# A hybrid encoder trunk on one core: another opening program, square sums one step later, set-up matrices at other places of the gate loop

## The chip, the cores and the metric

The kernel runs on one core of a Trainium2 chip. The metric is the device time of one execution in microseconds (us). TensorE multiplies, VectorE (DVE) and ScalarE (ACT) work on 128-partition tiles, GpSimd (POOL) does small side work, SyncE (SP) issues most DMAs. Each engine runs its own program in order and meets the others only at semaphores.

## The reference, cut to what matters

Two layers, 512 tokens, width 1024, all in float32.

```python
for l in range(DEPTH):                       # DEPTH = 2
    h = h + 0.5 * rms_norm(swiglu(rms_norm(h, g[0]), gate1, up1, down1), g[1])
    h = h + rms_norm(hybrid_mixer(rms_norm(h, g[2]), ...), g[3])
    h = h + 0.5 * rms_norm(swiglu(rms_norm(h, g[4]), gate2, up2, down2), g[5])

def rms_norm(x, g):
    return x * rsqrt(mean(x * x, -1) + 1e-6) * g
def swiglu(x, w_gate, w_up, w_down):         # 1024 -> 2816 -> 1024
    return (silu(x @ w_gate) * (x @ w_up)) @ w_down
```

The mixer has one input projection, a sliding-window attention, an S5 state-space layer, a forgetting attention, three branch norms and an output projection. The S5 layer's parameters are small: from `lam_re`, `lam_im`, `log_dt` it needs per state

```python
dt = exp(log_dt); mag = exp(min(lam_re, -1e-4) * dt)
ab_re = mag * cos(lam_im * dt);  ab_im = mag * sin(lam_im * dt)
z = ((ab_re - 1) + i ab_im) / (lam_re + i lam_im)      # scales B
```

The kernel turns them into matrices of powers of `ab`, so that the scan runs over chunks of 8 tokens. These matrices are made once per layer, beside the first FFN of the layer.

## The kernel before

**Layout.** Activations stand transposed: `hT[p, d, t]`, eight tiles d of 128 channels by 512 tokens. Every float32 product is made of three matmuls on split operands: a value is rounded to a high part (`xh`, `wh`, `Hh`) and a low remainder (`xl`, `wl`, `Hl`), and the product is xh·wh + xl·wh + xh·wl.

**A unit** is one weight tile: 1024 input channels by 128 output channels (512 KB). SyncE loads it into one of four raw slots. ScalarE rounds it (`split`, L914 to L918), VectorE makes the low part (`low`, L1334 to L1338), TensorE then runs its 24 matmuls (`unit_x`, L505, with L501 to L503 in `three`). A unit may be split when the unit two before it is done. Unit 2f of an FFN is the gate tile f, unit 2f + 1 the up tile f.

**The start of a stage.** `first_four` (L512) runs the first four units together, over the input tiles k as they come: `FIRST` lists (k tiles, units) for each step. Before its last two steps it runs `pre_norm` (L535): one fp32 matmul of ones with `acc`, the sum of the squares of h over the eight tiles, which ScalarE (`Square`, L955) and VectorE (`pre_sum`, L1355 to L1363) made. From it ScalarE makes `rstd` (`root`, L928 to L932). The input is not multiplied by `rstd`; the products are, in the gate function.

**The gate function** (`silu` on VectorE, L1405; `sigmoid` on ScalarE, L992) is a chain that goes back and forth between the two engines: L1407, ACT L996, L998, L1000, DVE L1411, ACT L1004, DVE L1416, L1418, then `times_up` L1423 with the up tile, ACT L1008 (`high`), DVE L1430 (`low_h`). The splits and lows of later units are placed between them by hand. In an FFN ramp unit 9's low half stands behind the fourth chain.

**Set-up of the S5 matrices** runs inside FFN 1 of each layer. GpSimd loads B and C, makes small powers and `bbar` and releases `z_bb` (`ssm_setup`). VectorE runs 12 `powers_step`s (L1456), each one instruction on 128x1024: they stand behind the pieces of `four` (L1474), the first at piece 10 (`POWER_AT`). TensorE runs six `ssm_matrix` steps (L555) behind the units of `STEP_UNIT`; ScalarE copies their results out (L967) three pieces later, at the end of the piece.

**The opening.** SyncE loads x as one DMA, then eight parameter transfers, then weights. TensorE waits for all of them, transposes x through PSUM (L491) and the parameters (L496, L497). ScalarE copies the eight tiles to `hT` (L898), converts two constants (L900, L901), and works on the S5 scalars with VectorE (L903 to L912, L1292 to L1331). Then both split the first four weight tiles, and make `xh` (L949) and `xl` (L1352).

## Time and profile before

Three timed runs took 2057.76 (median), 2057.37 and 2064.17 us. The profiled execution took 2057.29 us; its span, from the first to the last instruction that the profile counts, is 2055.5 us.

| engine | busy us | share of the span |
|---|---|---|
| TensorE (PE) | 1962.5 | 95% |
| VectorE (DVE) | 1128.1 | 55% |
| ScalarE (ACT) | 882.0 | 43% |
| GpSimd (POOL) | 208.8 | 10% |

A timeline row reads: start, duration, engine, line, operation, what is written and read, shape, count, and in brackets how long the engine was idle before it and what released it. Durations of pipelined instructions overlap, so the step from start to start is what counts. PEclk is TensorE's granted clock, 1.00 for 2.4 GHz and 0.50 for 1.2 GHz.

### The profile page before, as it was taken

How to read it: one execution, taken by the hardware profiler on the slowest of the kernel's cores; microseconds unless marked ns; L12 is line 12 of the kernel's file. 1: busy time of each engine (PE TensorE's matmuls, PEld its weight loads, DVE VectorE, ACT ScalarE, POOL GpSimd, SP SyncE). 2: the span in 40 equal slices, each digit the busy share in tenths (PEclk: the TensorE clock that was granted, in tenths of full speed). 3: DMA queues.
4: the chain of work that ended last, by engine and by line, in shares of the span. 5: the costliest groups of instructions: out<-in, count | busy, mean ns of one | idle time of the engine just before them, and what ended most of it. 6: DMA issues, size and time to landing. Idle time of an engine off the chain costs nothing.

```text
span 2055.5 us, 25149 instructions
## 1 busy us (share of the span) xinstructions
PE 1962.5 (95%) x9068; PEld 1565.1 (76%) x9068; DVE 1128.1 (55%) x1597; ACT 882.0 (43%) x1398; POOL 208.8 (10%) x409
## 2 busy tenths in 40 slices
PE   5999999999889999999999999999988999999997
PEld 4787888877657788888877788887765777888885
DVE  4674553377555755552277645325865576555323
ACT  4544442254554554442254444323555445444221
POOL 6502000012100000000057010000120000000000
PEclk9999999999989999999999999999999999999998
DMA  5324343252113233333332343333411123333321
GB/s 158 92 83 126 101 119 92 66 147 85 52 35 89 62 103 92 102 108 99 88 91 84 106 119 101 112 93 89 154 32 52 42 82 92 93 99 106 101 82 41
DMA packets 330427, 188.53 MB, mean 92 GB/s; under 512 B 6981, under 2 KB 325417, under 8 KB 329321
## 3 DMA queue, kind: packets, MB, share of 16 engines
q1 hardware_dynamic: 324520, 168.65, 28.5%
q0 software_dynamic: 5824, 18.79, 3.0%
q8 instruction: 50, 0.82, 0.2%
q14 instruction: 33, 0.26, 0.0%
HBM read 175.72 MB, written 11.67 MB: 91 GB/s over the span
## 4 chain that ended last, share of the span: by engine, by line
PE 74%; DVE 14%; ACT 8%; issue 3%; DMA 0%; SPq 0%; DVEq 0%; ACTq 0%
PE ps L501 13%; PE ps L502 13%; PE ps L503 13%; PE ps L632 8%; PE ps L634 8%; PE ps L633 8%; DVE wl L1337 3%; ACT wh L918 2%; DVE hT L1398 2%; PE ps L781 2%; PE ps L738 1%; DVE acc L1363 1%; PE ps L730 1%; DVE yF L1396 1%; ACT sig L998 1%
## 5 line engine op out<-in xcount | busy, mean ns | idle before, releaser
L1337 DVE TENSOR_TENSOR wl<-raw,wh 128x1024 fp32r<-128x1024 f32 (+1 forms) x270 | 356.3, 1320 | 519.5 <-ACT wh L918 518.3
L501 PE MATMUL ps<-xh,wh 128*128 128x512 f32 x1552 | 614.7, 396 | 11.0 <-DVE wl L1337 11.0
L502 PE MATMUL ps<-xl,wh 128*128 128x512 f32 x1552 | 607.5, 391 | 0.0
L503 PE MATMUL ps<-xh,wl 128*128 128x512 f32 x1552 | 607.5, 391 | 0.0
L918 ACT ACTIVATE wh<-raw 128x1024 fp32r<-128x1024 f32 (+1 forms) x270 | 304.9, 1130 | 443.7 <-PE ps L634 341.0
L501 PEld LDWEIGHTS ps<-xh,wh 128*128 128x128 f32 x1552 | 293.6, 189 | 80.5 <-DVE wl L1337 15.5
L503 PEld LDWEIGHTS ps<-xh,wl 128*128 128x128 f32 x1552 | 293.1, 189 | 62.3
L502 PEld LDWEIGHTS ps<-xl,wh 128*128 128x128 f32 x1552 | 293.7, 189 | 58.9
L632 PE MATMUL ps<-Hh,wh 128*128 128x512 f32 x704 | 278.3, 395 | 0.0
L634 PE MATMUL ps<-Hh,wl 128*128 128x512 f32 x704 | 278.0, 395 | 0.0
L633 PE MATMUL ps<-Hl,wh 128*128 128x512 f32 x704 | 277.9, 395 | 0.0
L632 PEld LDWEIGHTS ps<-Hh,wh 128*128 128x128 f32 x704 | 132.7, 189 | 32.4 <-DVE wl L1337 1.7
L634 PEld LDWEIGHTS ps<-Hh,wl 128*128 128x128 f32 x704 | 132.7, 188 | 31.0
L633 PEld LDWEIGHTS ps<-Hl,wh 128*128 128x128 f32 x704 | 132.7, 189 | 30.6
L1008 ACT ACTIVATE Hh<-full 128x512 fp32r<-128x512 f32 (+1 forms) x88 | 55.7, 632 | 228.0 <-DVE full L1423 217.5
L1411 DVE SCALAR_TENSOR_TENSOR sig<-sig 128x512 f32<-128x512 f32 x88 | 61.4, 697 | 130.2 <-ACT sig L1000 130.2
L996 ACT ACTIVATE sig<-sig 128x512 f32<-128x512 f32 x88 | 55.6, 632 | 147.3 <-DVE sig L1407 147.3
L1416 DVE TENSOR_TENSOR sig<-sig 128x512 f32<-128x512 f32 x88 | 62.0, 705 | 53.1 <-ACT sig L1004 53.1
L1004 ACT ACTIVATE sig<-sig 128x512 f32<-128x512 f32 x88 | 55.4, 630 | 57.8 <-DVE sig L1411 57.8
L1136 ACT ACTIVATE probT<-ps 128x256 f32<-128x256 f32 (+3 forms) x64 | 31.3, 489 | 84.6 <-PE ps L758 84.6
L1000 ACT ACTIVATE sig<-sig,ones 128x512 f32<-128x512 f32 x88 | 63.7, 724 | 2.9
L1418 DVE TENSOR_TENSOR sig<-sig,rstd 128x512 f32<-128x512 f32 x88 | 62.6, 712 | 3.0
(298 smaller groups left out, 2073.0 us busy)
## 6 DMA issues: line engine op xcount, KB each, us to landing
raw<-in_ffn_gate SPq DMA_DIRECT2D x88, 512.0 KB, 3.9
raw<-in_ffn_up SPq DMA_DIRECT2D x88, 512.0 KB, 3.9
raw<-in_ffn_down SPq DMA_DIRECT2D x64, 704.0 KB, 4.6
raw<-in_w_in SPq DMA_DIRECT2D x28, 512.0 KB, 4.0
raw<-in_w_out SPq DMA_DIRECT2D x16, 512.0 KB, 4.0
yF<-in_x SPq DMA_DIRECT2D x1, 2048.0 KB, 9.9
ssm_t<-evict POOLq DMA_DIRECT2D x8, 256.0 KB, 4.3
ssm_v<-evict POOLq DMA_DIRECT2D x8, 256.0 KB, 2.7
```

Of the source, the lines that this page charges most:

```text
L501: pe.matmul(bank, w_tile(True, slot, kw), xh[:, kx, :], start=first, stop=False)
L502: pe.matmul(bank, w_tile(True, slot, kw), xl[:, kx, :], start=False, stop=False)
L503: return pe.matmul(bank, w_tile(False, slot, kw), xh[:, kx, :], start=False, stop=last)
L632: pe.matmul(bank, wh[:, slot, k, :], Hh[:, f, :], start=(f == 0), stop=False)
L633: pe.matmul(bank, wh[:, slot, k, :], Hl[:, f, :], start=False, stop=False)
L634: mm = pe.matmul(bank, wl[:, slot, k, :], Hh[:, f, :], start=False, stop=(f == KF - 1))
L918: act.activation(w_high(slot, k0, nk), raw[:, slot4, 0:nk - k0, :], ACT.Copy).then_inc(w_hi, 1)
L1000: act.activation(e, e, ACT.Ln, bias=ones[:, 0:1]).then_inc(si_a, 1)
L1337: V.tensor_tensor(w_low(slot, k0, nk), raw[:, slot4, 0:nk - k0, :], w_high(slot, k0, nk).bitcast(F32), ALU.subtract).then_inc(w_split, 1)
L1411: V.scalar_tensor_tensor(e, g, 0.0, e, ALU.min, ALU.subtract).then_inc(si_v, 1)
L1416: V.tensor_tensor(e, g, e, ALU.mult).then_inc(si_v, 1)
L1418: V.tensor_tensor(e, e, rstd[:, :], ALU.mult).then_inc(si_v, 1)
```

## The change

- The first gate tile is loaded from ScalarE's queue. x comes in two halves, into memory of its own (`xrow`), with the gains and the identity between; weights 1 to 3 stand around the second half, and six late parameter transfers follow them.
- TensorE runs 12 small matmuls on constants first, transposes the gains and four tiles of x, and turns the other four tiles and the late parameters between the steps of a new order `FIRST0` of the first four units.
- ScalarE makes `xh` straight from PSUM; VectorE makes `xl` from PSUM and copies the tile to `hT`.
- The S5 scalars move: columns and angles on VectorE between the x tiles, the functions with their table loads and the two constant copies on ScalarE between weight split 4 and `root`, the inverse on VectorE behind the square sum, the 13 products to GpSimd. GpSimd's set-up of layer 0 starts when unit 0 is done.
- In all six ramps `pre_norm` stands before the last step in place of the last but one.
- The power steps start at piece 12 in place of 10; those of even pieces stand inside the gate function, behind `low_h`.
- ScalarE's matrix copies stand before the split of their piece in place of after its gate function or `high`.

```diff
-POWER_AT = 10
+POWER_AT = 12
+FIRST0 = (((0,), (0,)), ((0,), (1,)), ((1,), (0, 1)), ((0, 1), (2,)), ((2,), (0, 1, 2)), ((3,), (0, 1, 2)),
+          ((0, 1, 2, 3), (3,)), ((4,), (0, 1, 2, 3)), ((5,), (0, 1, 2, 3)),
+          ((6, 7), (0,)), ((6, 7), (1,)), ((6, 7), (2,)), ((6, 7), (3,)))
+X_TURN = {3: 4, 4: 5, 5: 6, 8: 7}
+P_TURN = 7
...
# SyncE
-            sp.dma_start(yF[:, :, :].rearrange("p (t a) n -> p t (a n)", t=TOK),
-                         x[0].rearrange("(t p) d -> p t d", p=P)).then_inc(s_in2, 16)
+            x_half(0)
+            sp.dma_start(par[0:96, 0, 0:P], norm_gains.rearrange("l g (k p) -> (l g k) p", p=P)).then_inc(s_in, 16)
             sp.dma_start(ident[:, :], const[:, K_ID:K_ID + P]).then_inc(s_in, 16)
...
+                    for i in range(4):
+                        if i == 2:
+                            x_half(1)
+                        if i:
+                            load(i, i, raw[:, i, 0:KD, :], columns((gate, up)[i % 2], l, slice(i // 2 * P, i // 2 * P + P)))
+                    late_params()
...
# TensorE
-            pe.wait_ge(s_in, 16 * 8)
-            pe.wait_ge(s_in2, 16)
+            pe.wait_ge(dve_c, 1)
+            for _ in range(SPIN_START):
+                pe.matmul(ps[0][:, 0:P], ones[:, :], ones[:, :], start=True, stop=True, skip_group_check=True)
+            def turn_x(k):
+                if k >= 4:
+                    pe.wait_ge(s_in2[1], 16)
+                    pe.wait_ge(h_new, k - 3)
                 if k == 7:
-                    pe.wait_ge(h_new, 1)
+                    pe.wait_ge(prm_rdy, 2)
...
+            def turn_params():
+                pe.wait_ge(s_set, 1)
+                pe.wait_ge(h_new, 4)
+                pe.transpose(ps[7][:, 0:R_C], par[0:R_C, 1, 0:P], ident[0:R_C, 0:R_C]).then_inc(s_set2, 1)
...
-                for step, (ks, us_) in enumerate(FIRST):
-                    if step == len(FIRST) - 2:
+                order = FIRST if s else FIRST0
+                for step, (ks, us_) in enumerate(order):
+                    if step == len(order) - 1:
                         pre_norm(s)
+                    if s == 0 and step in X_TURN:
+                        turn_x(X_TURN[step])
+                    if s == 0 and step == P_TURN:
+                        turn_params()
...
# ScalarE
+            act.dma_start(raw[:, 0, 0:KD, :], ffn1_gate[0:1, :, 0:P].rearrange("a (k p) f -> p (a k) f", p=P)).then_inc(landed[0], 16)
+            def ssm_functions():
+                act.wait_ge(s_ssm, 2)
+                act.activation(ssm[:, 4, :], ssm[:, 4, :], ACT.Exp).then_inc(s_act0, 1)
+                act.wait_ge(s_ssm, 3)
+                act.activation(ssm[:, 8, :], ssm[:, 7, :], ACT.Sin).then_inc(s_act0, 1)
+                act.activation(ssm[:, 9, :], ssm[:, 7, :], ACT.Sin, scale=0.5).then_inc(s_act0, 1)
+                act.add_instruction(mybir.InstLoadActFuncSet(...))
+                act.activation(ln_t[:, :], eps_t[:, :], ACT.Ln).then_inc(act_c, 1)
+                act.activation(maskb[:, :], maskf[:, :], ACT.Copy).then_inc(act_c, 1)
+                act.activation(identb[:, :], ident[:, :], ACT.Copy).then_inc(act_c, 1)
...
                 split_ahead(s, fourth(s) + 1)
+                if s == 0:
+                    ssm_functions()
                 act.wait_ge(pre_mm, s + 1)
                 root(ps[PRE_BANK][:, :], D_MODEL, rstd[:, :], ln_rdy, s * 2 + 1, pre_r)
...
                     for i in range(i0, 4):
+                        if i in step_of:
+                            ssm_matrix(l, step_of[i])
                         split(j * 4 + (n0 + i), j + n0 // 4, i, gu_slot(4 + i), KD)
...
-                        if i in step_of:
-                            ssm_matrix(l, step_of[i])
...
+            split_ahead(0, 0)
             act.wait_ge(prm_rdy, 1)
+            for k in range(KD):
+                x_start(k)
+                if k < 4:
+                    if k != 2:
+                        split_ahead(0, (1, 2, 0, 3)[k])
...
# VectorE
+            def x_start(k):
+                src = ps[4 + k % 4][:, :]
+                dve.wait_ge(x_hi, k + 1)
+                V.scalar_tensor_tensor(xl[:, k, :], src, prm[:, k:k + 1], xh[:, k, :].bitcast(F32),
+                                       ALU.mult, ALU.subtract).then_inc(x_rdy, 1)
+                V.tensor_copy(hT[:, k, :], src).then_inc(h_new, 1)
+            low_ahead(0, 0)
+            for k in range(KD):
+                x_start(k)
+                if k in (0, 1, 3):
+                    low_ahead(0, (1, 2, 0, 3)[k])
+                if k == 3:
+                    spread()
+                if k == 5:
+                    ssm_columns()
+            ssm_angles()
...
                 pre_sum(s)
+                if s == 0:
+                    ssm_inverse()
                 low_ahead(s, 4)
...
+                        def between():
+                            low_h(f + (tiles - 1), 1 - fb, bass.ds(f - 1, 1))
+                            if 0 <= step < 12:
+                                powers_step(step)
                         if i % 2 == 0:
                             dve.wait_ge(unit_done, n - 2 + SPLIT_SLOTS + 1)
-                            silu(f + tiles, b, lambda: low_h(f + (tiles - 1), 1 - fb, bass.ds(f - 1, 1)))
+                            silu(f + tiles, b, between)
                         else:
                             times_up(f + tiles, fb, b, n - 2)
-                        if set_up and 0 <= 4 * j + i - POWER_AT < 12:
-                            powers_step(4 * j + i - POWER_AT)
+                            if 0 <= step < 12:
+                                powers_step(step)
...
# GpSimd
-                if l:
-                    await_(unit_done, l * U_LAYER + SPLIT_SLOTS)
+                await_(unit_done, l * U_LAYER + SPLIT_SLOTS + 1 - (1 if l else 0))
...
                 if l == 0:
-                    await_(s_ssm, 4)
+                    ssm_products()
```

## Rows read from the trace of the kernel before

**Rows 1.** The page's chain by engine, and TensorE's waits (total us, times, longest).

```profile
PE 74%; DVE 14%; ACT 8%; issue 3%; DMA 0%; SPq 0%; DVEq 0%; ACTq 0%
...
PE ps L501 <- DVE wl L1337: 11.0, 13, 2.0
...
PE ps L538 <- DVE acc L1363: 4.9, 5, 1.0
...
PE ps L569 <- ACT evict L983: 4.0, 4, 1.4
```

**Rows 2.** Timeline of TensorE, 10 to 51 us (columns as told above).

```profile
12.19 1.12 PE L491 MATMUL ps<-ident,yF 128*128 128x128 f32 x4 [12.19 <-DMA full<-const]
...
29.18 0.77 PE L526 MATMUL ps<-xh,wh 128*128 128x512 f32 x1 [11.40 <-DVE wl L1337]
...
50.26 1.02 PE L538 MATMUL ps<-acc,ones 128*128 128x512 f32 x2
```

**Rows 3.** Timeline of ScalarE and VectorE, 18 to 42 us.

```profile
18.52 0.57 ACT L900 ACTIVATE maskb<-full 128x384 bf16<-128x384 f32 x1
...
19.76 0.21 ACT L905 ACTIVATE ssm<-ssm 128x16 f32<-128x16 f32 x1 [0.38 <-DVEq L1300]
...
21.67 1.28 ACT L910 ACT_TABLE_LOAD   x1
...
23.07 1.04 ACT L918 ACTIVATE wh<-raw 128x1024 fp32r<-128x1024 f32 x1
...
35.29 0.68 DVE L1360 TENSOR_TENSOR acc<-sq 128x512 f32<-128x512 f32 x1
...
36.66 4.68 DVE L1363 TENSOR_TENSOR acc<-acc,sq 128x512 f32<-128x512 f32 x6 [0.70 <-ACT sq L955]
```

**Rows 4.** Windows of SyncE: stretch, length, PEclk, DMA share, GB/s.

```profile
2.00:7.00 5.00, 1.00 1.02 329
...
12.00:18.00 6.00, 1.00 1.18 279
```

**Rows 5.** Timeline of TensorE in the ramps of the FFNs and behind the set-up.

```profile
82.37 0.50 PE L501 MATMUL ps<-xh,wh 128*128 128x512 f32 x1 [1.10 <-DVE wl L1337]
...
96.13 0.50 PE L501 MATMUL ps<-xh,wh 128*128 128x512 f32 x1 [1.99 <-DVE wl L1337]
...
194.00 0.39 PE L501 MATMUL ps<-xh,wh 128*128 128x512 f32 x1
...
199.44 0.39 PE L501 MATMUL ps<-xh,wh 128*128 128x512 f32 x1
...
713.62 0.50 PE L501 MATMUL ps<-xh,wh 128*128 128x512 f32 x1 [0.67 <-DVE wl L1337]
...
1055.25 1.13 PE L538 MATMUL ps<-acc,ones 128*128 128x512 f32 x2 [0.98 <-DVE acc L1363]
...
1100.38 0.50 PE L501 MATMUL ps<-xh,wh 128*128 128x512 f32 x1 [1.70 <-DVE wl L1337]
...
1198.70 0.39 PE L501 MATMUL ps<-xh,wh 128*128 128x512 f32 x1
```

**Rows 6.** Timeline of VectorE, 91 to 103 us: gate chain and power step.

```profile
91.00 0.69 DVE L1411 SCALAR_TENSOR_TENSOR sig<-sig 128x512 f32<-128x512 f32 x1 [1.52 <-ACT sig L1000]
...
93.72 1.22 DVE L1468 TENSOR_TENSOR prod<-bbar,pw_b 128x1024 f32<-128x1024 f32 x1
...
102.27 0.69 DVE L1411 SCALAR_TENSOR_TENSOR sig<-sig 128x512 f32<-128x512 f32 x1 [1.52 <-ACT sig L1000]
```

**Rows 7.** TensorE's small matmuls, and the window behind them (PE, PEld, DVE, ACT, POOL, PEclk).

```profile
176.13 4.21 PE L577 MATMUL ps<-cT,bbd 64*128 64x16 f32 x64 [1.68 <-ACT evict L983]
...
180.30:188.50 8.20, 8.20 (x25) 6.53 (x25) 0.00 (x0) 0.00 (x0) 0.00 (x0) 0.65 0.37 98
```

**Rows 8.** Timeline of GpSimd, start and end of its first chain.

```profile
25.60 1.11 POOL L1870 TENSOR_TENSOR wk<-ssm 128x8 f32<-128x8 f32 x1 [5.76 <-DVEq L1331]
...
51.46 0.19 POOL L1890 COPY wk<-ssm 128x8 f32<-128x8 f32 x1
```

More of the change, by code:

```diff
@@ L331, in build @@
         s_in = sem("params_landed")
-        s_in2 = sem("input_rows_landed")
+        s_in2 = [sem(f"input_half{i}_landed") for i in range(2)]
+        s_par = sem("late_params_landed")
         s_small = sem("sinks_and_bias_landed")
@@ L438, in ffn_loads @@
             def ffn_loads(l, base_gu, base_down, gate, up, down):
-                with sp.Fori(0, KF // 2) as j:
+                first = l == 0 and base_gu == U_GU1
+                if first:
+                    for i in range(4):
[4 more added lines that the diff above has]
+                    late_params()
+                with sp.Fori(1 if first else 0, KF // 2) as j:
                     for i in range(4):
@@ L946, in pre_norm @@
                 l, pi = s // 3, s % 3
-                for d in range(KD):
+                for d in range(KD if s else 0):
                     act.wait_ge(h_new, s * KD + d + 1)
@@ new lines, in ssm_columns, with ssm_angles @@
+            def ssm_columns():
+                dve.wait_ge(s_set2, 2)
+                link(V.tensor_copy(s(LDT), ps[7][:, R_LDT:R_LDT + 16]))
+                dve.sem_inc(s_ssm, 1)
+                link(V.tensor_scalar(s(LR), ps[7][:, R_LRE:R_LRE + 16], -1e-4, None, ALU.min))
+                link(V.tensor_copy(s(LI), ps[7][:, R_LIM:R_LIM + 16]))
+                link(V.tensor_copy(prm[:, 96:R_A], ps[7][:, R_B:R_C]))
+                dve.sem_inc(prm_rdy, 1)
+            def ssm_angles():
+                dve.wait_ge(s_act0, 1)
+                tt(MAG, LR, DT, ALU.mult)
+                dve.sem_inc(s_ssm, 1)
+                tt(TH, LI, DT, ALU.mult)
+                link(V.tensor_scalar(s(KK).bitcast(I32), s(TH), 1.0 / (2 * np.pi), None, ALU.mult))
+                link(V.tensor_copy(s(T1), s(KK).bitcast(I32)))
+                C1 = 6.28125
+                C2 = float(np.round((2 * np.pi - C1) * 2.0 ** 20) / 2.0 ** 20)
+                C3 = float(2 * np.pi - C1 - C2)
+                for c in (C1, C2, C3):
+                    link(V.scalar_tensor_tensor(s(TH), s(T1), -c, s(TH), ALU.mult, ALU.add))
+                PI = float(np.nextafter(np.float32(np.pi), np.float32(0)))
+                link(V.tensor_scalar(s(RR), s(TH), PI, -PI, ALU.min, ALU.max))
+                dve.sem_inc(s_ssm, 1)
@@ L1334, in low, with ssm_inverse @@
+            def ssm_inverse():
+                tt(T1, LR, LR, ALU.mult)
+                tt(T2, LI, LI, ALU.mult)
+                tt(DEN, T1, T2, ALU.add)
+                link(V.reciprocal(s(DEN), s(DEN)))
+                dve.sem_inc(s_ssm, 1)
+                dve.wait_ge(s_small, 32)
+                link(V.tensor_scalar(nsinks[:, :, :], sinks[:, :, :], -1.0, None, ALU.mult))
             def low(n, slot4, slot, nk, k0=0):
@@ L1781, in mixer, with x_start @@
                 out_last(l, l * (3 * KD) + KD + 7, yM[:, 7, :], 7, 1.0, out_bank(7), 3)
[L1784 to L1787 removed]
+            def x_start(k):
+                src = ps[4 + k % 4][:, :]
[13 more added lines that the diff above has]
+            ssm_angles()
             for l in range(DEPTH):
```

150 lines of the change are left out of this document (65 added, 85 removed).

## The prediction

> **What bounds the kernel now.** I read the chain of waits first. TensorE holds 74% of it, and 3% is issue time [rows 1]. A gain is therefore time in which TensorE stands still, or runs at the lower of its two clock levels. Second came TensorE's own waits. It waits 13 times for VectorE's low halves of the weights, 11.0 us in all, and five times about 1 us at L538, the sum of the squares [rows 1]. Third came the timelines of the stretches that the diff touches. Three places lose time.
>
> 1. The opening. The first transpose is at 12.19, released by the last parameter transfer. The first real matmul is at 29.18, after 11.40 us of standing still; the first sum of squares (call its start T) is at 50.26 [rows 2].
> 2. The ramp of each FFN. Unit 9 (a unit is one tile of gate or up weights, 24 matmuls) starts at 82.37, which is T + 32.1. Unit 11 starts at 96.13 after 1.99 us of idle; in layer 1 it starts at 1100.38, and in FFN 2 unit 9 waits 0.67 [rows 5]. These starts come from the chain of gate functions, not from TensorE.
> 3. The set-up matrices inside FFN 1. A unit at full clock takes 199.44 - 194.00 = 5.44 (0.227 a matmul). From unit 11 to unit 26 are 15 units (81.6), five groups of four transposes (some 0.35 each, 1.8) and the 64 small matmuls (4.2): 87.6. The trace has 194.00 - 96.13 = 97.9 in layer 0 and 1198.70 - 1100.38 = 98.3 in layer 1, so 10.3 and 10.7 are lost [rows 5, 7].
>
> **Part 1, the opening.** Ahead of gate tile 2 (the third weight tile, and the last that stops the ScalarE queue early) now come 2.1 MB of x, 0.1 of gains and identity and 1.6 of weights, 3.8 MB. The trace moves 329 GB/s at 2 to 7 us and 279 at 12 to 18 [rows 4]. From 2 us on that is 13.6 to 15.6, and about 1 us for the landing; I take 15.6. The first x half, gains and gate tile 0 (1.7 MB) land near 8, so TensorE starts the first pieces near 10, but starves until ScalarE (1.04 [rows 3]) and VectorE (1.2, as the step of this size in [rows 6]) have split tile 2: 17.8. From there it has 48 matmuls (10.9) and four turns of parameters and x (some 0.6 each, 2.4; the first four transposes take 1.12 [rows 2]) to the eighth x tile, and 1.5 more for some 3 us at the lower clock: 32.6. ScalarE's tile 0.6, VectorE's xl and copy 1.3 (a 128x512 step is 0.68 [rows 3]), eight small angle steps 1.8 by estimate: the sums of squares start at 36.3. They take 35.29 to 41.34, 6.05 [rows 3]. So T becomes 42.4, 7.9 earlier, and it is VectorE that sets it: TensorE would be there near 39.6 and waits. The bounds are 39.0 (no stall, the clock up) and 46 (transfers at the older pace with its hole, parameters late).
>
> **Part 2, what was moved behind it.** ScalarE's functions (two table loads, sine, logarithm) and two copies ran at 18.52 to 23.07, before TensorE had work. Now they stand between weight split 4 and the root of the norm. From 19.76 to 23.07 is 3.3 and the copies 0.9 (0.57 for the larger): 4.2 [rows 3]. ScalarE would have been free about 1.0 before the root, so rstd comes 3.15 later after T. Everything of the gate chain queues behind it: unit 6 waits about 2, unit 9 starts at T + 35.2 in place of T + 32.1. The load is 1.28 in the trace, and the logarithm and the start of the next split lie within 0.12 of its end [rows 3]. The Trainium skill (ScalarE: Activation LUTs, What ACT_TABLE_LOAD costs) gives about 2.66 us with a drain; by that estimate two loads would put 2.8 more on this path and the sum at 2038.4. The trace does not agree, so I keep the row. VectorE's ssm_inverse (1.1) fits into its wait for rstd.
>
> **Part 3, the power matrices.** Unit 10's low half waited behind nothing, but unit 11's stood behind power step 0: 93.72 to 94.86, 1.14 [rows 6]. With the first step two pieces later unit 11 starts 11.8 after unit 9. Layer 0: 42.4 + 35.2 + 11.8 = 89.4 against 96.13, -6.7. Layer 1: -1.1. In later pairs the even step moves into the 1.52 us wait before L1411 [rows 6] and hides: 0.60 for the low half of H, 1.14 for the step, inside a wait that ends 2.2 after L1407's end. The chain of a pair falls from 11.27 (L1411 at 91.00 and 102.27 [rows 6]) to 10.1, below TensorE's 10.9, so the odd waits go. Step 0 of ScalarE's matrix copies costs 1.14 ahead of a split now, but VectorE has that 1.14 back there.
>
> **Part 4, ScalarE's matrix copies one half-piece earlier.** TensorE waits for ScalarE's copies four times at L569, 4.0 us, two in each layer [rows 1], and 1.68 before the small matmuls at 176.13 [rows 7]. Each copy now leaves before the split of its piece, some 4 us earlier, so all go. What is late next is the z_st store, off the path. The clock stays: after the small matmuls the granted clock is 0.65 for 8.2 us, which one unit fills in place of 5.44 [rows 7]. The idle ahead goes, but the 64 thin matmuls themselves keep the array little used, so I keep 2.0 of the 2.8 (bounds 0 and 2.8), and 0.7 for small waits. Parts 3 and 4 after unit 11: 10.3 - 2.7 = 7.6 and 10.7 - 2.7 = 8.0.
>
> **Part 5, the square sum one piece later in each ramp.** At 1055.25 TensorE had waited 0.98, 1.14 by starts [rows 5]. Six matmuls (1.4) now run there, so the wait goes and L538 starts 0.26 later. In the two mixers (TensorE-bound behind it) that is -1.1 each. In the FFN ramps the gate chain bounds units 9 and 11, so the 1.14 is only waited there, and the chain is 0.26 later: +0.26 in each FFN 2, and in layer 1's FFN 1. The idle before unit 9 grows to 3.4 in layer 0, 2.5 in layer 1 and 2.1 in each FFN 2 (0.67 + 1.14 + 0.26). At 96.13 an idle of 1.99 was followed by a stretch at the lower level: the unit behind it took some 7.2, 1.8 more than at the full one. I put +2.5 for the four together (bounds 0 and 6).
>
> **Sum.** -6.7 - 7.6 (layer 0), -1.1 + 0.3 - 8.0 (layer 1), -2.2 (mixers), +0.5 (FFN 2), +2.5 (clock) = -22.3. The profiled run took 2057.29 with a span of 2055.5; it lies 0.5 below the median, 2057.76. So 2035.0 by that run, 2035.5 by the median.
>
> **Rivals.**
> - *The lower clock eats it* (0.18). Longer idles before unit 9 in all four ramps and the whole 2.8 twice after the thin matmuls: +3.5 + 1.6, and T at 45: +2.6. Gives 2043. For it: 1.99 us was enough at 96.13. Against it: the wait at 1100.38, 1.70, was not.
> - *The opening is better than that* (0.15). Data land at once, the thin matmuls no longer drop the clock, T at 40: -2.4 - 4.0 - 1.0. Gives 2028. Against it: VectorE's queue alone takes 24 us from its first x tile.
> - *The opening gives nothing* (0.05), the change does not do what it says there: parameters, x and functions only change places, and rstd in layer 0 comes when it came. The 4.8 that unit 9 gains falls away, the rest stays: 2040.
> - *GpSimd becomes late* (0.03), the slower side. Its set-up in layer 0 starts only when unit 0 is done (near 37, in place of 10), with 10 us of issues and 13 products more; then its chain to the first matrix, 25.60 to about 50, 25 us [rows 8]. That gives z_bb near 80, and power step 0 wants it near 92. The first of its instructions takes 1.11 though, with VectorE busy beside it, against 0.19 for a later one on tiles of that size [rows 8]. If all of some 69 ran at 1.2 the first matrix would come at 47 + 83 = 130, step 0 would hold VectorE and every low half behind it 38 us, and the kernel takes 2035 + 38 = 2073. It costs from 92 on and makes the change slower from about 114. The Trainium skill (SBUF — State Buffer, Who interferes with whom) has this rule: a VectorE instruction with two SBUF inputs and a GpSimd one that reads SBUF lock each other out, and the power steps and low halves are of that kind. The trace bears it out for single instructions, not for all.
>
> **How the numbers follow.** Main case 0.59. Its own range is 2030 to 2041; with the rivals 2027 to 2046 holds 8 in 10. What a measurement of this kernel can tell from no change is about 0.5%, 10.3 us, so faster is below 2047.5. All cases but the last lie below it, but their sizes can be off together, for which I leave 0.05: faster 0.92, same 0.05, slower 0.03. The time is 2035.5.
>
> **What would show it.** T near 42 with TensorE waiting 2 to 3 us for VectorE's sum; two table loads between T and rstd and unit 6 late by 2; unit 11 near 89; no TensorE wait for ScalarE's evict, none for low halves in units 12 to 17; in the mixers no wait at the square sum, but more before unit 9 of each FFN. It is wrong if T is above 46 or below 39, if low halves are still late after unit 11 (GpSimd, or ScalarE's copies ahead of the split), or if the time is above 2046.

## The result, and the profile after

On one chip the changed kernel took 2029.46 us (median of 4 runs, 2028.45 to 2030.89), the kernel before 2058.32 (4 runs): ratio 0.9858, 95% interval 0.9837 to 0.988, so 28.9 us less. Taken again beside the third group of experiments below (a_again, a_open, a_best, a_thin) it was 2030.57 (4 runs, 2028.63 to 2034.05), ratio 0.9855 (0.984 to 0.987). The forecast was 2035.5, range 2027 to 2046: direction right, 5 to 6 us too slow. The experiments ran on two chips, and the kernel before ran beside each group: kernels of different groups are compared by their ratios to it and by the stretches of their profiles, not by their times.

The profiled execution took 2030.34 us with a span of 2028.4, against 2055.5 before. The page and TensorE's waits (line waited for: us in total, times, longest) answer to [rows 1]:

```profile
PE 82%; DVE 9%; ACT 6%; issue 2%; DMA 1%; SPq 0%; DVEq 0%; ACTq 0%
```

```profile
PE ps L541 <- DVE wl L1393: 11.4, 12, 1.8
...
PE ps L583 <- DVE acc L1419: 3.3, 1, 3.3
```

TensorE holds 82% of the chain instead of 74%. The wait for the square sum (L583, L538 before) is there once instead of five times, and the wait for ScalarE's evicts is gone from the list. But the waits for low halves are as large as before, 11.4 against 11.0: they went between units 12 and 17 and came back elsewhere. Where, the timeline of TensorE shows (it answers to [rows 2], [rows 5] and [rows 7]; L541 is L501 before, L622 is L577):

```profile
12.75 0.55 PE L571 MATMUL ps<-xh,wh 128*128 128x512 f32 x1
...
40.80 2.08 PE L583 MATMUL ps<-acc,ones 128*128 128x512 f32 x2 [3.31 <-DVE acc L1419]
...
67.95 0.47 PE L541 MATMUL ps<-xh,wh 128*128 128x512 f32 x1 [1.11 <-DVE wl L1393]
...
75.17 0.50 PE L541 MATMUL ps<-xh,wh 128*128 128x512 f32 x1 [1.52 <-DVE wl L1393]
...
87.11 0.50 PE L541 MATMUL ps<-xh,wh 128*128 128x512 f32 x1 [0.73 <-DVE wl L1393]
...
178.34 0.39 PE L541 MATMUL ps<-xh,wh 128*128 128x512 f32 x1
...
440.90 0.47 PE L541 MATMUL ps<-xh,wh 128*128 128x512 f32 x1 [0.85 <-DVE wl L1393]
...
697.32 0.50 PE L541 MATMUL ps<-xh,wh 128*128 128x512 f32 x1 [1.44 <-DVE wl L1393]
...
1070.98 0.50 PE L541 MATMUL ps<-xh,wh 128*128 128x512 f32 x1 [1.79 <-DVE wl L1393]
```

Real matmuls begin at 12.75 instead of 29.18. T is 40.80, behind a wait of 3.31 for VectorE, and its matmul takes 2.08 instead of 1.02: the granted clock fell there (0.62 from 40.8 to 44.5). 75.17 is unit 9 of layer 0, 87.11 unit 11, 178.34 unit 26. At 440.90, in the mixer, stands a wait that was not there before: the later square sum took one away, and it came back two units on.

To see where 28 us went, cut each trace at TensorE's unit starts (24 matmuls each). This table is the main instrument of what follows; its columns are starts or differences of starts in us, one profile a row. u is a unit; the columns behind u26 of layer 0 are "to the next T" and layer 1's FFN 1; the last runs to the end of the span.

| kernel | T | to u9 | u9 to u11 | to u18 | to u26 | to T (L1) | to u9 | u9 to u11 | to u18 | to u26 | rest |
|---|---|---|---|---|---|---|---|---|---|---|---|
| before | 50.3 | 32.1 | 13.8 | 41.2 | 56.7 | 861.2 | 32.3 | 12.9 | 41.6 | 56.7 | 856.8 |
| changed | 40.8 | 34.4 | 11.9 | 38.7 | 52.5 | 860.8 | 31.8 | 11.7 | 38.9 | 50.9 | 855.8 |
| changed, again | 42.3 | 34.2 | 12.1 | 38.7 | 51.0 | 861.5 | 31.8 | 11.7 | 39.0 | 52.6 | 857.3 |
| b_sum | 52.5 | 32.6 | 12.8 | 40.6 | 56.8 | 861.9 | 31.9 | 12.9 | 41.6 | 56.8 | 856.4 |
| b_pow | 50.6 | 32.1 | 12.6 | 38.7 | 57.2 | 858.2 | 32.2 | 11.7 | 39.0 | 55.6 | 857.7 |
| b_mat | 50.6 | 32.1 | 13.8 | 39.4 | 52.6 | 860.8 | 32.2 | 12.9 | 40.4 | 51.0 | 856.8 |
| b_three | 52.3 | 32.5 | 12.5 | 38.6 | 52.6 | 860.8 | 31.8 | 12.6 | 39.1 | 52.6 | 857.5 |
| a_func | 41.9 | 36.3 | 12.4 | 38.7 | 51.0 | 861.3 | 31.8 | 11.7 | 39.0 | 52.6 | 857.2 |
| a_ramp | 42.9 | 32.2 | 12.0 | 38.7 | 52.5 | 857.0 | 30.7 | 11.7 | 38.9 | 49.4 | 855.5 |
| a_spin0 | 42.6 | 34.4 | 11.9 | 38.7 | 51.0 | 860.6 | 31.8 | 11.7 | 38.9 | 52.6 | 854.4 |
| a_spq | 43.5 | 34.4 | 11.9 | 38.7 | 49.4 | 859.5 | 31.8 | 11.7 | 39.0 | 50.9 | 855.7 |
| a_open | 39.6 | 31.5 | 12.4 | 39.0 | 50.9 | 860.2 | 31.8 | 11.7 | 38.9 | 52.6 | 854.3 |
| a_best | 40.3 | 30.7 | 12.5 | 38.7 | 52.6 | 859.5 | 30.8 | 11.8 | 39.0 | 49.4 | 854.8 |
| a_thin | 41.4 | 34.4 | 11.9 | 38.7 | 49.7 | 860.6 | 31.8 | 11.7 | 38.9 | 49.7 | 857.0 |

Most columns repeat within 0.2 between kernels with the same edits. Four don't: T (40.8 to 43.5 with the same opening), "to u26" (steps of about 1.6), and the two long stretches (up to 5). Each of them holds stretches in which TensorE's granted clock differs from profile to profile: see b_pow for a long one, a_again for T, and the last section for "to u26".

### The profile page after: what moved, and what is told of

Same layout as the page of the kernel before. It is cut to its first block, busy times and chain, and to the rows that moved or that the text cites. A ratio compares the mean times of both kernels' runs of the same rounds, so it can differ in the third digit from the quotient of the medians.

```text
span 2028.4 us, 25214 instructions
## 1 busy us (share of the span) xinstructions
PE 1960.5 (97%) x9092; PEld 1564.1 (77%) x9092; DVE 1132.5 (56%) x1593; ACT 877.1 (43%) x1390; POOL 215.2 (11%) x422
## 4 chain that ended last, share of the span: by engine, by line
PE 82%; DVE 9%; ACT 6%; issue 2%; DMA 1%; SPq 0%; DVEq 0%; ACTq 0%
PE ps L541 15%; PE ps L542 15%; PE ps L543 15%; PE ps L677 8%; PE ps L678 8%; PE ps L679 8%; DVE wl L1393 2%; PE ps L576 2%; ACT wh L961 2%; PE ps L571 2%; PE ps L572 2%; PE ps L826 2%; PE ps L775 1%; PE ps L783 1%; PE ps L803 1%
## 5 line engine op out<-in xcount | busy, mean ns | idle before, releaser
L541 PE MATMUL ps<-xh,wh 128*128 128x512 f32 x1552 | 613.8, 395 | 11.5 <-DVE wl L1393 11.4
L541 PEld LDWEIGHTS ps<-xh,wh 128*128 128x128 f32 x1552 | 293.1, 189 | 81.8 <-DVE wl L1393 12.2
L1055 ACT ACTIVATE Hh<-full 128x512 fp32r<-128x512 f32 (+1 forms) x88 | 55.6, 632 | 211.6 <-DVE full L1479 211.6
L1043 ACT ACTIVATE sig<-sig 128x512 f32<-128x512 f32 x88 | 55.6, 632 | 147.9 <-DVE sig L1463 147.9
L1463 DVE TENSOR_TENSOR sig<-ps,rstd 128x512 f32<-128x512 f32 x88 | 60.2, 684 | 8.6 <-PE ps L576 4.5
```

The source lines that it names most:

```text
L541: pe.matmul(bank, w_tile(True, slot, kw), xh[:, kx, :], start=first, stop=False)
L1463: V.tensor_tensor(g, ps[2 * b][:, :], rstd[:, :], ALU.mult).then_inc(si_v, 1)
```

## Experiments: the change taken apart

**b_sum.** The kernel before, with Part 5 alone.

```
-                    if step == len(FIRST) - 2:
+                    if step == len(FIRST) - 1:
                         pre_norm(s)
```

> The kernel before with one edit: the sum-of-squares matmul stands ahead of the last piece instead of the last but one, in all six ramps. By the prediction's Part 5: the waits of about 1 us at L538 in the five ramps that had one go; each mixer gains 1.1, each FFN 2 loses 0.26 and layer 1's FFN 1 0.3: -1.4 in all, and the first ramp, which had no wait there, loses 0.5 at most. By my reading of the two traces (additive theory): the mixers give back most of it to the low half two units later, the FFN ramps gain 0.2 each: -1.3 to -1.9. Both end near 2057; what tells them apart is the place: under the prediction unit 9 of FFN 2 comes later against the mixer's end by 0.26, under the reading 0.2 earlier, and the mixer's third unit behind the ramp waits for its low half. Rival: the square sum's place does nothing at all (within 0.3), the wait is only moved.

2055.97 us (12 runs; 17 of before, 2058.99), ratio 0.9987 (0.9977 to 0.9997): 0.6 to 5 us less. The two profiles can't show that: the profiled execution was one of the slower of the 12 (2058.42), that of the kernel before one of its faster (2057.29), spans 2056.6 and 2055.5. Its timeline of TensorE:

```profile
85.04 0.79 PE L501 MATMUL ps<-xh,wh 128*128 128x512 f32 x1 [2.49 <-DVE wl L1337]
...
458.31 0.47 PE L501 MATMUL ps<-xh,wh 128*128 128x512 f32 x1 [0.83 <-DVE wl L1337]
...
714.82 0.50 PE L501 MATMUL ps<-xh,wh 128*128 128x512 f32 x1 [1.47 <-DVE wl L1337]
```

The waits at the sum turn into one of 0.83 at the mixer's unit 6, and the 0.67 before unit 9 of FFN 2 becomes 1.47. In layer 0 the sum comes 2.2 later, unit 9 waits 2.49, and the unit behind it runs at the lower level: its first matmuls take 0.63 instead of 0.39. Unit 18 of layer 0 starts 1.2 later than before, and from unit 26 to the mixer's unit 8 it is 276.7 instead of 276.4. So the stretches explain none of the gain that the 12 runs have, and where it comes from is open.

**b_pow.** The kernel before, with Part 3 alone.

```
-POWER_AT = 10
+POWER_AT = 12
...
+                        def between():
+                            low_h(f + (tiles - 1), 1 - fb, bass.ds(f - 1, 1))
+                            if 0 <= step < 12:
+                                powers_step(step)
-                            silu(f + tiles, b, lambda: low_h(f + (tiles - 1), 1 - fb, bass.ds(f - 1, 1)))
+                            silu(f + tiles, b, between)
```

> The kernel before with the power matrices alone changed: the first of twelve steps at unit 12 instead of 10, and the even steps inside the wait between a gate function's first product and its exponential. By the prediction's Part 3: unit 11's wait shrinks by 1.14 in both layers, and the waits for low halves in units 12 to 17 go (0.51 in layer 0, 0.43 + 0.28 + 1.25 in layer 1); ScalarE's matrix copies still cost their 3.7 a layer. That is 1.14 + 0.51 and 1.14 + 1.96, so -4.8. Theory A (the clock at unit 11 fell because its idle was 1.99 long): with 0.85 left there the stretch behind it stays at the full level and gives 1.65 more: -6.4. Theory B (it fell for what came before, the waits at 82.37 and 88.42): the clock still falls, -4.8. Rival C: with the low halves on time TensorE runs ahead and waits longer for ScalarE's copies instead, so that only the 1.14 of each layer and the clock come through: -2.3 to -4.

2048.2 us (6 runs), ratio 0.9946 (0.9934 to 0.9958): -10.8, more than any theory gave. The stretches say what is in it. Unit 9 to 11 is 1.14 shorter in both layers, as predicted, and to unit 18 it is 2.5 and 2.6 shorter. Of layer 0's 2.5, 1.65 is clock: the wait before unit 11 is 0.87, and the unit behind it takes 5.57 (95.35 to 100.92) instead of 7.22 (96.13 to 103.35). That is as theory A had it; b_mat shows that it was not the idle's length alone. The 3.0 in the long stretch of layer 0 has no cause in the edit: it is the granted clock, in one place of the mixer. Windows (start and end, length, busy us of PE, PEld, DVE, ACT, POOL with counts, then PEclk, DMA share, GB/s) of the same 36 us of work, in the kernel before and in b_pow:

```profile
578.00:614.00 36.00, 33.83 (x152) 22.67 (x151) 24.03 (x52) 21.05 (x48) 0.00 (x0) 0.85 0.13 33
```

```profile
575.20:611.20 36.00, 33.74 (x171) 22.79 (x170) 24.13 (x52) 22.03 (x50) 0.00 (x0) 0.94 0.18 52
```

In the windows beside these the two have the same clock within 0.01. Over the whole stretch from the mixer's unit 8 to the next square sum it is 0.97 in b_pow, a_ramp and a_spq (208.5 to 209.7 us) and 0.95 in the kernel before and the changed one (211.5). By the stretches from unit 9 to unit 18 alone b_pow gains 7.4, 1.65 of it clock; what else the six runs have is open.

**b_mat.** The kernel before, with Part 4 alone.

```
                     for i in range(i0, 4):
+                        if i in step_of:
+                            ssm_matrix(l, step_of[i])
                         split(j * 4 + (n0 + i), j + n0 // 4, i, gu_slot(4 + i), KD)
...
-                        if i in step_of:
-                            ssm_matrix(l, step_of[i])
```

> The kernel before with ScalarE's copies of the set-up matrices alone moved, ahead of the split of their place instead of behind the gate function. By the prediction's Part 4: all waits for these copies go, 3.68 and 3.67 us in the two layers, and of the clock loss behind the 64 thin matmuls 0.8 each: -9.0 together, less what the low halves behind the power steps then ask (0.5 to 2). By my reading of the two traces: -7.4 for the waits and 0.4 of the clock, so -7.8. Rival: without the power steps' move VectorE's low halves are late in the same units (they wait for a split that now stands behind a copy), TensorE waits for them instead, and less than half comes through: -4 or less.

2043.8 us (6 runs), ratio 0.9921 (0.9908 to 0.9934): -15.2, by the spans -13.0, more than any theory gave. All evict waits go, and the 0.51 and 1.25 before unit 17 shrink to 0.06 and 0.08 with the power steps still in their old place. From unit 11 to unit 26 it is 5.9 and 7.0 less; 1.6 of the 5.9 is the clock at unit 11, which the edit does not touch. What is left, 11.2, is the 7.4 of evict waits, the 1.6 at unit 17 and 2.2 more; 1.6 of that lies at the thin matmuls of layer 1, where unit 23 to 24 takes 9.21 instead of 12.49 and the wait that went was 1.68. This is about half of the change's gain, in two lines that move.

```profile
96.45 0.50 PE L501 MATMUL ps<-xh,wh 128*128 128x512 f32 x1 [1.99 <-DVE wl L1337]
...
102.04 0.39 PE L501 MATMUL ps<-xh,wh 128*128 128x512 f32 x1
```

The same idle of 1.99 us before unit 11 as in [rows 5], and here the clock did not fall (1.00 from 96.5 to 102): 5.59 to the next unit.

**b_three.** Parts 3, 4 and 5 on the old opening.

> The kernel before with the three edits together and its old opening: all of the change but the opening and what was moved behind it. The additive theory (offsets of unit starts in the two traces): unit 9 to 11 -1.8, unit 11 to 26 -6.6 in layer 0, -1.1 and -8.5 in layer 1, mixers and FFN 2 -1.6 to -1.9: -19.9, near 2038.4, so the opening is worth 7.2. The prediction's terms without its Parts 1 and 2: -1.1 - 7.6 - 1.1 + 0.3 - 8.0 - 2.2 + 0.5 = -19.2 and up to +2.5 of clock. Rival: the opening is worth much less than 7.2 (or more), because the first ramp of the old opening profits more from the later square sum or from the power steps; then this kernel ends below 2035 or above 2042.

2043.29 us (5 runs), ratio 0.9913 (0.9898 to 0.9928); span 2042.9. Not better than b_mat alone. The median is above the rival's 2042, but the interval, 2038.0 to 2044.2 by the ratio, holds the additive 2038.4 too, so the time does not decide between them. By the ratios the opening adds 11 to 12 us to it, give or take 5, where the theory had 7.2. Two things made it slow, both in its TensorE timeline:

```profile
84.87 0.79 PE L501 MATMUL ps<-xh,wh 128*128 128x512 f32 x1 [2.48 <-DVE wl L1337]
...
1081.20 0.66 PE L501 MATMUL ps<-xh,wh 128*128 128x512 f32 x1 [1.82 <-DVE wl L1337]
...
1081.66 0.63 PE L502 MATMUL ps<-xl,wh 128*128 128x512 f32 x1
```

In the old opening the later square sum costs T 2.1 us and unit 9 2.5 (84.87 against 82.37), since TensorE was the bound there (no wait before T). In the new one TensorE waits 3.3 before T anyway, so the same edit should be free; that was not run by itself. And the clock falls behind both idles, 1.5 to 1.6 a time (7.10 and 7.15 to the next unit instead of 5.57; PEclk 0.71 behind each).

## Experiments: the opening

**a_func.** The changed kernel with ScalarE's functions in the wait for the first H tile, and the two mask copies behind the ramp.

```
                 split_ahead(s, fourth(s) + 1)
-                if s == 0:
-                    ssm_functions()
                 act.wait_ge(pre_mm, s + 1)
...
+                        if l == 0 and f_ffn == 0:
+                            ssm_functions()
                         act.wait_ge(unit_done, n0 + 3 + SPLIT_SLOTS + 1)
                         high(tiles, 0, bass.ds(0, 1))
```

> The changed kernel with ScalarE's sine, logarithm and their two table loads moved out of the stretch between the first sum of squares (T) and the root, into the wait before the first H tile, and the two mask copies behind the ramp. In the trace of the changed kernel the root starts at 44.60 and the sum's matmul is over near 42. The prediction's Part 2 says that the functions and copies cost the ramp 3.15 us: rstd then comes 3.15 earlier after T; 3.3 us of functions stand in an idle of 2.37, which gives 1.0 back: unit 9 earlier by 2.1. Rival A (trace of the kernel with the three edits and the old opening: unit 9 at T + 32.5, in the changed one at T + 34.4): the price is only 1.8, so less 1.0, unit 9 earlier by 0.8. Rival B: GpSimd's set-up starts some 8 us later, its first matrix comes near 84 instead of 75.5, still ahead of power step 0 near 92; if it is late instead, TensorE waits for low halves from unit 13 on and the kernel is slower.

2033.12 us (5 runs), ratio 0.9878 (0.9859 to 0.9896): slower than the changed kernel by 4 to 5 by the ratios, with intervals that overlap. Unit 9 is at T + 36.3, 2 later instead of earlier, and unit 26 is 2.0 to 2.1 later. All theories missed it; ScalarE's timeline says why:

```profile
43.80 0.69 ACT L971 ACTIVATE rstd<-ps,eps_t 128x512 f32<-128x512 f32 x1 [0.60 <-PE ps L583]
44.51 1.28 ACT L973 ACT_TABLE_LOAD   x1
45.80 0.63 ACT L973 ACTIVATE rstd<-rstd 128x512 f32<-128x512 f32 x1
...
48.59 1.28 ACT L1043 ACT_TABLE_LOAD   x1
...
50.63 1.28 ACT L1047 ACT_TABLE_LOAD   x1
```

The moved block held the load of the table that has both exponential and logarithm. Without it the root and the first gate function each switch between two tables: four loads more (the first, at 41.92, lies in the root's wait for TensorE). The edit tested its own mistake, not Part 2. a_open has the load in front.

**a_open.** The changed kernel with the wait that its own trace shows filled: VectorE stands 3.03 us for the parameters' transpose, ScalarE 7.51 for the last x tile. The functions go ahead of the squares, the mask copies behind the ramp.

```
-X_TURN = {3: 4, 4: 5, 5: 6, 8: 7}
-P_TURN = 7
+X_TURN = {3: 4, 4: 5, 5: 6, 7: 7}
+P_TURN = 6
...
                 if k == 5:
                     ssm_columns()
-            ssm_angles()
+                    ssm_angles()
...
+            ssm_functions()
...
-                if s == 0:
-                    ssm_functions()
```

> The changed kernel with its opening reordered: parameters turned one step earlier, the last x tile one step earlier, VectorE's angles and ScalarE's functions with their two table loads ahead of the squares' chain, in the waits of 3.0 (VectorE) and 7.5 us (ScalarE) that the trace of the changed kernel shows at 24 to 31, and the mask copies behind the ramp. Theory (the prediction's Part 2: VectorE sets T, and the functions between T and the root hold rstd): T at 38.2 (6.05 of sums behind the last x tile at 30 to 31), TensorE waits under 1 us for it in place of 3.3 and keeps its clock, rstd at T + 2.6 in place of T + 5.1, unit 9 of layer 0 near T + 32.5 = 70.7 against 75.2: -4.5, kept to unit 26. Rival: the table loads now fall between the x tiles and hold the squares, so T stays near 41 and only rstd gains: -2.5. Second rival: GpSimd or the chain of gate functions (not rstd) sets unit 9: less than -1.

2028.07 us (5 runs), ratio 0.9844 (0.9831 to 0.9858): 2.5 less than the changed kernel beside it, by the spans 5.4 to 9.1; the intervals overlap, so the time alone does not settle it. The stretches do: unit 9 starts at 71.18 instead of 75.17 and 76.46, and unit 26 at 173.51 instead of 178.34 and 178.20, the 4.5 of the theory. ScalarE, first in the changed kernel, then in a_open:

```profile
40.95 1.28 ACT L948 ACT_TABLE_LOAD   x1
...
42.58 1.28 ACT L951 ACT_TABLE_LOAD   x1
...
44.60 0.67 ACT L973 ACTIVATE rstd<-ps,eps_t 128x512 f32<-128x512 f32 x1
```

```profile
29.18 1.28 ACT L946 ACT_TABLE_LOAD   x1
...
30.82 1.28 ACT L949 ACT_TABLE_LOAD   x1
...
40.80 0.69 ACT L969 ACTIVATE rstd<-ps,eps_t 128x512 f32<-128x512 f32 x1 [1.14 <-PE ps L583]
```

The root starts at T + 1.2 instead of T + 3.8, and unit 9 is at T + 31.5 instead of T + 34.2 to 34.4: the functions and copies cost the ramp 2.7 to 2.8. T itself came only to 39.64 (I had 38.2), behind a wait of 1.55, since the first squares now queue behind the second load and VectorE stands 2.69 for them: a part of the rival.

**a_spin0, a_spq.** The changed kernel without its 12 early matmuls, and with gate tile 0 on SP's queue.

> The changed kernel without the 12 small matmuls on ones at its start (1.54 to 6.6 us in its trace). The prediction put 1.5 us for a lower clock in the opening; the trace has none between 9 and 37 us. Theory A: the early matmuls had raised the clock, without them the transposes and first pieces (9.4 to 16) run at the lower level and T comes 0 to 1 later, since VectorE sets T. Theory B: the clock rises by itself within the first transposes, T is the same within 0.3.

> The changed kernel with the load of gate tile 0 on SP's queue, behind the first half of x, gains and identity, instead of on ScalarE's. The transfers share the engines and bring 380 to 400 GB/s between 4 and 8 us either way: theory A, what is ahead of tile 0 counts, not the queue: tile 0 lands last, 0.5 to 1.5 later than at 9.9, the gains earlier; T, set by VectorE's queue behind low half 0, is 0.5 to 1.5 later. Theory B: the queue of SP issues it late (three issues ahead of it, each some 0.5): the same 1.5. Theory C, bandwidth alone: all land together near 9.5, T within 0.3.

2030.94 and 2032.5 us (2 runs each), both medians within the changed kernel's own runs; one run of a_spq, 2036.5, is not. T was 42.59 and 43.52. TensorE's first real matmul in a_spin0, and in a_spq:

```profile
12.68 0.77 PE L571 MATMUL ps<-xh,wh 128*128 128x512 f32 x1 [1.00 <-DVE wl L1393]
13.24 0.63 PE L572 MATMUL ps<-xh,wl 128*128 128x512 f32 x1
```

```profile
6.83 0.41 PE L534 MATMUL ps<-ident,par 96*128 96x96 f32 x1
...
12.81 0.47 PE L571 MATMUL ps<-xh,wh 128*128 128x512 f32 x1 [3.53 <-DVE wl L1392]
```

With tile 0 on SP's queue the gains are turned at 6.83 (9.36 in the first profile of the changed kernel, 7.56 in its repeat) and the first split is at 10.39 instead of 9.90; the first matmul is at 12.81, against 12.75, and 11.75 in the repeat below. T was the latest of all with this order of the opening, 1.3 behind the repeat, as theories A and B had it, but T spreads by 2.1 without the edit (40.80 to 42.88), so one profile does not settle the queue. The data did not come as I had it: 279 GB/s from 4 to 8 us in the changed kernel and 258 in a_spq, not 380 to 400. Without the early matmuls the first pieces run at the lower level by their steps (0.43 from 15.61 to 19.02 for what takes 0.23 at the full one, though the recorded granted clock says 1.00 there), as theory A had it, but so they do in the repeat, so T tells nothing here. Nor was the changed kernel's own trace free of it: its granted clock was 0.50 from 10 to 12 us, and its 16 transposes took 3.58 where the repeat took 1.91.

**a_again.** The changed kernel, unaltered.

> The changed kernel itself, unaltered, once more. In its first profile T (first sum of squares) was at 40.80; the kernels of the second group, whose opening is the same on VectorE, had it at 41.9 to 43.5. Theory A: 40.80 was the early end of a spread of 1 to 2 us that comes from when the first weight tile lands and at which clock the first pieces run; T here is near 42.4, as predicted, unit 26 of layer 0 is within 0.5 of 178.3 all the same or up to 1.6 later. Theory B: T is a property of the program: 40.8 within 0.3. The time is within 3 us of 2029.5 in both.

```profile
11.75 0.47 PE L571 MATMUL ps<-xh,wh 128*128 128x512 f32 x1 [2.15 <-DVE wl L1393]
...
14.10 0.80 PE L571 MATMUL ps<-xh,whx 128*128 128x512 f32 x1 [1.23 <-DVE wlx L1393]
14.69 0.63 PE L572 MATMUL ps<-xh,wlx 128*128 128x512 f32 x1
...
42.26 1.13 PE L583 MATMUL ps<-acc,ones 128*128 128x512 f32 x2 [3.32 <-DVE acc L1419]
```

Theory A, for the clock and not for tile 0, which is early here. TensorE waits 2.15 and 1.23, runs at the lower level from 14.10 to 19.8 (PEclk 0.50; 1.00 in the first profile from 13 on), and T is 42.26. How that reaches T, ScalarE's row of the last x tile shows, in the first profile and in the repeat:

```profile
30.67 0.69 ACT L1284 ACTIVATE xh<-ps,prm 128x512 fp32r<-128x512 f32 x1 [7.51 <-PE ps L523]
```

```profile
32.12 0.69 ACT L1284 ACTIVATE xh<-ps,prm 128x512 fp32r<-128x512 f32 x1 [7.51 <-PE ps L523]
```

ScalarE waits for TensorE to turn that tile, and T comes 10.13 us behind this start in all seven profiles with this order (30.67 to 33.39, T 40.80 to 43.52). So VectorE sets T, with TensorE waiting 3.3 in each, only from the last x tile on; up to it TensorE's own pieces do, and the whole spread of T arises there.

## Experiments: the ramp and the clock

**a_ramp.** One edit on VectorE, in all four FFN ramps.

```
                         if f == 0:
                             low_ahead(s, 5)
+                        if f == 1:
+                            low_unit(n0 + 6, gu_slot(6))
...
                     times_up(fn, f % 2, gu_pair(f), n0 + 2 * f + 1)
-                    if f == 0:
-                        low_unit(n0 + 6, gu_slot(6))
```

> The changed kernel with one edit on VectorE in the ramp of every FFN: the low half of unit 6 behind the first product of the second gate function instead of ahead of it. In the changed kernel VectorE waits 1.71 for the split of unit 6 and then takes 1.2 for its low half before the second gate function starts. Theory (the chain of gate functions sets units 8, 9 and 11, not VectorE's load and not the low halves' own length): the chain is 2.0 us earlier from the second function on; the waits before unit 9 (1.44 in each FFN 2, 1.79 in layer 1's FFN 1, 1.11 + 1.52 in layer 0's) go, and nearly all of those before unit 11: -1.8 in each FFN 2, -2.2 and -2.5 in the two FFN 1, -8.3 together. Rival: TensorE's units 8 and 9 wait for their slots' splits (ScalarE), the waits stay over half their length: -3 or less. It also tells on Part 5 of the prediction: if the ramps' waits go, the square sum's later place is paid back there.

2025.56 us (5 runs), ratio 0.9843 (0.9823 to 0.9863), against 0.9858 and 0.9855 for the changed kernel: the intervals overlap, and of the 6.7 by which its span is below the first profile's about 3 is the mixer's clock (0.97 for 0.95) and 1.5 that of unit 18 to 26 in layer 1. What the edit does is read from the stretches. T to unit 9 is 32.2 instead of 34.3 in layer 0 and 30.7 instead of 31.8 in layer 1; before unit 9 of FFN 2:

```profile
693.58 0.50 PE L541 MATMUL ps<-xh,wh 128*128 128x512 f32 x1 [0.66 <-DVE wl L1393]
```

0.66 in place of 1.44. So the chain of gate functions does set these starts, but half the wait stays: -1.1 in each FFN 2 and in layer 1's FFN 1 and -2.1 in layer 0, 5.4 together where I had 8.3.

**a_best.** a_open and a_ramp together.

> The reordered opening and the ramp edit (low half of unit 6 behind the second gate function's first product) together. If both mechanisms hold: layer 0 gains 4.5 to 6 against the changed kernel (with the ramp's chain 2 earlier, nothing waits before units 8 and 9), the two FFN 2 0.8 each and layer 1's FFN 1 0.7 as measured in the ramp kernel by the starts of unit 9, less chance of a fall of the clock behind them: 6.8 to 8.5 less than the changed kernel, near 2022. Rival: the gains of layer 0 do not add (TensorE is the bound there once one of the two is made), -5 in all.

2020.62 us (5 runs, 2017.79 to 2023.9), ratio 0.9809 (0.9795 to 0.9822): 10.0 less than the changed kernel beside it, and the two intervals do not touch. Expected were 6.8 to 8.5 less. Unit 9 of layer 0 is at T + 30.7, 0.8 below a_open, so of the ramp's 2.1 there 0.8 is left beside the other edit; in layer 1 all of it is (30.8). It beats both kernels.

**a_thin.** The changed kernel with 32 of the 64 thin matmuls behind unit 23 and 32 behind unit 24.

```
-STEP_UNIT = {12: 0, 18: 1, 19: 2, 20: 3, 21: 4, 23: 5}
+STEP_UNIT = {12: 0, 18: 1, 19: 2, 20: 3, 21: 4, 24: 5}
...
-                    for t in range(ST):
+                    for t in range(half * ST // 2, (half + 1) * ST // 2):
...
+                        if isinstance(j, int) and f_ffn == 0 and j * 4 + i == 23:
+                            ssm_matrix(l, 5, 0)
```

> The changed kernel with the 64 thin matmuls cut in two: 32 behind unit 23, 32 behind unit 24, and ScalarE's copies of their result one unit later. The stretch from unit 18 to unit 26 took 49.4, 51.0 or 52.6 us in all kernels with the copies ahead of the split, so the fall of the clock behind them cost 0, 1.6 or 3.2. Theory A (the prediction's Part 4: the thin matmuls themselves, 4.6 us with the array little used, bring the clock down): 2.3 us at a time do it less or not at all, 49.4 to 51.0 in both layers, -1 to -4 in the time. Theory B (any thin stretch does it, or the idle of the low halves around it): two falls instead of one, 52.6 or more, 0 to +3. Theory C: the fall has nothing to do with them and comes at any time; the stretch takes 49.4 here and the 1.6 turns up elsewhere.

2028.77 us (5 runs), ratio 0.9847 (0.9834 to 0.9861): 1.8 less, within the intervals. The stretches are plain: unit 18 to 26 takes 49.7 in both layers. Windows (columns as at b_pow) of a_thin in layer 0, and of the changed kernel again in both layers:

```profile
155.00:163.00 8.00, 8.00 (x60) 6.64 (x59) 4.23 (x6) 4.42 (x6) 1.70 (x3) 1.00 0.83 280
163.00:171.00 8.00, 8.00 (x58) 6.69 (x59) 3.58 (x5) 1.90 (x3) 0.00 (x0) 1.00 0.24 68
```

```profile
166.00:173.00 7.00, 7.00 (x26) 5.58 (x25) 0.34 (x1) 0.96 (x3) 4.80 (x7) 0.76 0.45 98
1161.00:1170.00 9.00, 9.00 (x31) 7.24 (x32) 0.35 (x1) 1.32 (x4) 6.82 (x9) 0.68 0.49 94
```

The granted clock stays at 1.00, in layer 1 too, where it was 0.76 and 0.68. So it is the 64 thin matmuls at a stretch that bring it down, not an idle ahead of them, of which the changed kernel has none; two stretches are few, since 3 of 20 did not fall with 64 either.

## Why the prediction was right, and by how much off

- **Part 1, T at 42.4:** measured 40.8, and 42.3 in the repeat, inside 39 to 46. The steps of the working came out one by one: the first product with tile 2 at 17.79 and 18.81 (17.8 foreseen), the last x tile at ScalarE at 30.67 and 32.12 (32.6 foreseen), T 10.1 behind it (9.8 foreseen), TensorE's wait 3.3 (2 to 3). "VectorE that sets it" holds from the last x tile on; before that TensorE does. The 1.5 for the lower clock came in the repeat alone, and that is the difference between the two.
- **Part 2:** the two loads took 1.28 each, as the trace had it. The Trainium skill (ScalarE: Activation LUTs, What ACT_TABLE_LOAD costs) gives about 2.66 us for a switch, with a drain, so 5.3 for two by that estimate. The traces show no drain: every load, the changed kernel's two and a_func's six, takes 1.28, and the next activation starts within 0.12 us of its end unless it waits for another engine. The sum with it would be 2035.5 + 2.8 = 2038.3, not 2038.4. Unit 9 is at T + 34.3 instead of T + 35.2: the price of 3.15 was 2.7 to 2.8 (a_open), and unit 6 waited 0.1 and 1.2, not 2.
- **What was off in the sum: "unit 11 at 89.4, -6.7".** It was 87.1 and 88.5, -9.0 and -7.6: T 1.6 and 0.1 early, T to unit 9 0.8 and 1.0 shorter than 35.2, unit 9 to 11 11.9 and 12.1 for 11.8. That 11.8 is partly luck. The rows of layer 0 give 13.8 less 1.14, so 12.6, which is what b_pow measured on the old opening; that it is 11.9 behind the new one no term of the working says, and no run isolates why.
- **Parts 3 and 4, -7.6 and -8.0 behind unit 11:** -6.6 and -8.5, in the repeat -8.2 and -6.8; the mean of the four is -7.5. The size is right; how it splits was not tested before. Part 4 alone brings -5.9 and -7.0 of it (1.6 of the 5.9 by chance, see b_mat), Part 3 alone -1.9 and -3.7 and the -1.1 at unit 11; on top of Part 4, Part 3 has 0.9 and 1.3 left from unit 11 to unit 18 (b_three against b_mat).
- **Part 5, -2.2 in the mixers, +0.8 in the ramps:** wrong in the mixers. "The wait goes" was right, "TensorE-bound behind it" was not: unit 6 then waits 0.83 to 0.85 for its low half, so from unit 26 to the mixer's unit 8 it is 276.2 (once 276.7) instead of 276.4. In layer 1's ramp and in FFN 2 unit 9 comes about 0.2 earlier, not 0.26 later. By the stretches the edit is worth about nothing; b_sum's runs, with 0.6 to 5 us less, do not quite agree.
- **Clock, +2.5 in the ramps:** not incurred. The idles before unit 9 that it was put on, 3.4, 2.5 and 2.1, came as 1.5, 1.8 and 1.4, with another 1.1 before unit 8 in layer 0, and no fall came behind them in either profile. One came behind the 3.3 before T in the first (its sum took 2.08 instead of 1.02); T to unit 9 is 34.4 with it and 34.2 without, so it cost next to nothing. The kept 2.0 of 2.8 behind the thin matmuls was 1.6 or 3.1.
- **The sum, by the spans:** -22.3 was forecast, the first profile has -27.1, the repeat -23.4. In the first, 2.5 of the 4.8 that were missed are the clock and 2.3 the way to unit 11. In the repeat two misses hide each other: the clock's 2.5 did not come, and the long stretches, forecast at -1.7, came at +0.8. So a part of the closeness there is luck.
- **Rivals.** GpSimd's last product on the first matrix, in its timeline:

```profile
73.90 1.52 POOL L1909 TENSOR_TENSOR bbar<-bbar,ptmp 128x128 f32<-128x128 f32 x1
```

  It ends at 75.4, before the 80 of the working, and no low half waits for it. In time the best-opening rival (2028) came nearest: 2029.46 is just below the main case's own range of 2030 to 2041, 2030.57 in it. Of its three conditions T near 40 held in the first profile alone, and the thin matmuls did bring the clock down.

The long stretches behind unit 26, where the square sum's place is the only edit, differ by up to 5 us between profiles, with the mixer's clock in them (b_pow). Their share of the 28 (0.4 and 1.0 here) I cannot give to any part.

## What to carry to other kernels

An instruction queued ahead of work that others wait for costs its length and the wait in front of it: moving ScalarE's copies one place was worth more than any other part by the stretches (11.2 us in the two layers without the chance clock), and it is found by asking for each wait what stands before it in the late engine's queue. A wait that goes comes back at the next late operand: follow it three units on before it is counted. Edits are not additive across a change of the bound: price each against the version in which it will stand.

## What the runs showed of the hardware

The loss of clock comes in steps. In the ten profiles that have ScalarE's copies ahead of the split and 64 thin matmuls at a stretch (nine kernels, the changed one twice), unit 18 to unit 26 took, in two layers each, 49.4 three times, 50.9 to 51.0 seven times and 52.5 to 52.6 ten times, at the same instructions: 0, 1.55 or 3.1 us lost. Elsewhere a fall cost 1.65 (unit 11 before) and 1.5 to 1.6 (unit 9 in b_sum and b_three), and one place of the mixer costs 3 us more in some profiles than in others (b_pow). Whether it falls is not fixed by the length of the idle ahead: 1.99 did it once (before) and not once (b_mat), 1.82 not in b_sum and once in b_three, 2.48 and 2.49 both times, the 3.31 before T in five of seven profiles with the same opening, none at 1.44 to 1.81 in the ramps. A fall does not always cost time at the end: behind T it is made up in the waits before units 6 and 8. Any single profile of such a kernel is uncertain by 3 us and more for that alone; cutting it at fixed points of the work tells an edit of 1 us all the same. What decides whether it falls stays open.
